# Gate products ahead of up products, the router's fold moved to GpSimd, and constant products in TensorE's waits

## The reference

```
mod = silu(c) @ W_ada + b_ada              -> shift, scale, gate, twice
h   = rms_norm(x)*(1+sc1) + sh1
u   = h @ W_in                             -> SSD group | MLA group
SSD : causal conv, SiLU, chunked scan (8 chunks of 128 tokens, 8 heads)
MLA : low-rank q and kv, rotary part, causal softmax attention, 8 heads
x   = x + g1 * rms_norm(concat(SSD, MLA) @ W_out)
h   = rms_norm(x)*(1+sc2) + sh2
router: group = argmax of 4 logits; the best 2 of that group's 8 experts
x   = x + g2 * rms_norm(sum over the 2 experts of
          w_e * (silu(h @ W_gate[e]) * (h @ W_up[e])) @ W_down[e])
```

## Time and profile before

| What | us |
|---|---|
| median of 3 runs | 1045.89 |
| fastest and slowest of them | 1043.03, 1046.33 |
| the profiled execution | 1050.27 |
| its span, first to last instruction | 1048.5 |
| TensorE busy in it | 954.7 |
| VectorE, ScalarE, GpSimd busy | 520.2, 302.3, 204.9 |

### The profile page before, as it was taken

The page is one execution under the profiler, slowest core; times in us unless marked ns, Lnnn a source line. Parts: engine busy times, 40 slices in busy tenths (PEclk is TensorE's granted clock), DMA queues, the critical chain, the costliest instruction groups (busy, mean ns, idle before and its releaser), DMA issues. The chain is left out here.

```text
span 1048.5 us, 12759 instructions
## 1 busy us (share of the span) xinstructions
PE 954.7 (91%) x4459; PEld 505.9 (48%) x4459; DVE 520.2 (50%) x961; ACT 302.3 (29%) x585; POOL 204.9 (20%) x247
## 2 busy tenths in 40 slices
PE   6999999999999999987999999748999998999946
PEld 4444444445466656666566665433333333333312
DVE  3366356444755555555578775662333332333327
ACT  3310001223443434432322322103333332333313
POOL 2200001223400600003343312011222221222003
PEclk9999999999989999998999999858999999999979
DMA  9986423000000000004011112995999999997547
GB/s 341 374 324 214 159 82 51 0 1 6 1 1 1 2 1 1 1 21 180 20 62 67 75 60 93 404 385 192 363 419 391 415 406 399 403 413 317 203 198 295
DMA packets 51815, 192.40 MB, mean 183 GB/s; under 512 B 15322, under 2 KB 20514, under 8 KB 36258
## 3 DMA queue, kind: packets, MB, share of 16 engines
q1 hardware_dynamic: 43396, 173.10, 42.6%
q0 software_dynamic: 7056, 18.36, 4.6%
q10 hardware_dynamic: 1296, 0.07, 0.1%
HBM read 174.21 MB, written 24.64 MB: 190 GB/s over the span
## 5 line engine op out<-in xcount | busy, mean ns | idle before, releaser
L1607 PE MATMUL PS<-ring,xg_T 128*64 x368 | 165.2, 603 | 3.5 <-ACT near_gu L1784 2.6
L1607 PE MATMUL PS<-near_gu,xg_T 128*64 128x512 f32 x368 | 165.2, 603 | 0.0
L1506 PE MATMUL PS<-w_out_sb,cat_T 128*128 128x512 f32 x256 | 120.8, 614 | 4.1 <-DVE y_sc L1927 2.8
L1003 PE MATMUL PS<-hT,w_x 128*128 128x512 f32 x256 | 111.6, 594 | 0.7 <-DMA w_x<-in_w_in_dram 0.7
L1607 PEld LDWEIGHTS PS<-ring,xg_T 128*64 128x64 f32 x368 | 51.1, 140 | 109.8 <-issue 109.8
L425 POOL TENSOR_SCALAR rstd<-stat 128x1 f32<-128x1 f32 (+1 forms) x48 | 21.9, 457 | 383.4 <-ACT junk L593 187.7
L1633 PE MATMUL PS<-ring,hid_T 128*64 x184 | 83.8, 598 | 0.4 <-DVE hid_T L2142 0.4
L1633 PE MATMUL PS<-near_dn,hid_T 128*64 128x512 f32 x184 | 83.9, 599 | 0.0
L2133 DVE TENSOR_TENSOR hid<-PS,hid_s 128x128 f32<-128x128 f32 x46 | 11.3, 286 | 145.9 <-ACT hid_s L1766 145.8
L898 DVE TENSOR_REDUCE row_max<-PS 128x1 f32<-128x1024 f32 (+7 forms) x64 | 48.2, 753 | 65.6 <-PE PS L1178 65.5
L1176 PE MATMUL PS<-kT,qT 96*128 96x512 f32 (+4 forms) x192 | 78.4, 519 | 0.0
(11 more groups left out here) (333 smaller groups left out, 1527.4 us busy)
## 6 DMA issues: line engine op xcount, KB each, us to landing
ring<-in_w_gate_dram SPq DMA_DIRECT2D x32, 1024.0 KB, 8.9
ring<-in_w_up_dram SPq DMA_DIRECT2D x32, 1024.0 KB, 11.7
ring<-in_w_down_dram SPq DMA_DIRECT2D x32, 1024.0 KB, 16.9
ada_later<-in_ada_w_dram SPq DMA_DIRECT2D x16, 1024.0 KB, 4.8
ada_first<-in_ada_w_dram SPq DMA_DIRECT2D x16, 512.0 KB, 10.7
y_g<-y_rows SPq DMA_DIRECT2D x8, 1024.0 KB, 12.4
x_in<-in_x_dram SPq DMA_DIRECT2D x8, 512.0 KB, 9.1
w_x<-in_w_in_dram SPq DMA_DIRECT2D x4, 1024.0 KB, 15.6
```

Source lines behind the costliest of these rows:

```text
L1003: last = pe.matmul(BANK[4 + n % 4][:, :], w_x[:, k, ct * P:(ct + 1) * P], hT[:, k, hh * HALF:(hh + 1) * HALF], start=(k == 0), stop=(k == ...
L1506: last = pe.matmul(BANK[6 + j], cat_T[t % 2][:, k, :], w_out_sb[:, k, j * HALF:(j + 1) * HALF], start=(k == 0), stop=(k == KC - 1))
L1607: last = pe.matmul(BANK[2 + b][rows_, :], xg_T[b][:, k, rows_], gu[u][:, :, k, :], start=(k == 0), stop=(k == KC - 1))
```

## The change

**The fold.** `router_columns`, `router_row` and their copies on VectorE are gone. GpSimd does the fold during attention, behind the chunk decays: the row times the identity, broadcast, and a tree of additions that leaves the diagonal as columns; the same with the 36 columns of the shift's product. What is left to TensorE is one product with `ones`, behind the first two products of the second block, and VectorE adds its result to the bias row there.

**Constant products.** `busy(bank, n)` issues n products of the identity with `ones` (128x128) into a bank that nothing reads before it is written again. In the lead-in there are 32 of them in six places, in the routing 105 in five (20, 4, 21, 24, 36).

**Gate and up.** `gate_up` does 16 products of 256 columns for gate into bank 2, and signals `gate_done`, then 16 for up into bank 3. SiLU waits for `gate_done`, the multiplication for `gu_done` as well. Both banks are now used by every tile; before, tiles took turns between two. So the next tile's gate waits for SiLU, and its up for the multiplication.

The diff (lists of semaphore names and unchanged lines left out):

```diff
@@ -213,6 +213,8 @@
+        fold = place("fold", R_U + 4096, [P, KC, P])
+        fold_r = place("fold_r", R_U + 4096, [P, KC, NG + E])
@@ -498,6 +500,22 @@
+            pool.wait_ge(S["w_r_loaded"], 32)
+            pool.wait_ge(S["mod_rows_ready"], 4 * (PARTS - 1))
+            for i, v in enumerate((B2, A2)):
+                link(pool.tensor_tensor(fold[:, :, :], v[:, :].rearrange("p (j k) -> p k j", k=KC), ident[:, :].unsqueeze(1).to_broadcast([P, KC, P]), ALU.mult))
+                n = P // 2
+                while n > 1:
+                    link(pool.tensor_tensor(fold[:, :, 0:n], fold[:, :, 0:n], fold[:, :, n:2 * n], ALU.add))
+                    n //= 2
+                link(pool.tensor_tensor(modc[:, i * KC:(i + 1) * KC].unsqueeze(2), fold[:, :, 0:1], fold[:, :, 1:2], ALU.add))
+            by_channel = lambda c0: modc[:, c0:c0 + KC].unsqueeze(2).to_broadcast([P, KC, NG + E])
+            link(pool.tensor_tensor(fold_r[:, :, :], w_r[:, :, :], by_channel(0), ALU.mult))
+            n = KC // 2
+            while n:
+                link(pool.tensor_tensor(fold_r[:, 0:n, :], fold_r[:, 0:n, :], fold_r[:, n:2 * n, :], ALU.add))
+                n //= 2
+            pool.tensor_tensor(w_r[:, :, :], w_r[:, :, :], by_channel(KC), ALU.mult).then_inc(S["fold_pool"], 1)
@@ -881,9 +899,6 @@
-                if hh == NH2 - 1:
-                    dve.wait_ge(S["fold_pe"], 1)
-                    dve.tensor_copy(modc[:, :], BANK[4][:, 0:2 * KC]).then_inc(S["fold_dve"], 1)
@@ -897,11 +912,6 @@
-                if st == 0:
-                    dve.wait_ge(S["fold_pe"], 2)
-                    dve.wait_ge(S["fold_dve"], 1)
-                    dve.tensor_tensor(rb_row[:, :], BANK[5][:, 0:NG + E], rb_row[:, :], ALU.add).then_inc(S["fold_dve"], 1)
-                    dve.tensor_tensor(w_r[:, :, :], w_r[:, :, :], modc[:, KC:2 * KC].unsqueeze(2).to_broadcast([P, KC, NG + E]), ALU.mult)
@@ -1087,22 +1097,6 @@
-            def router_columns():
-                pe.wait_ge(S["v_read"], NT - 1)
-                for i, v in enumerate((B2, A2)):
-                    for k in range(KC):
-                        last = pe.transpose(BANK[4][:, i * KC + k:i * KC + k + 1], v[0:1, k::KC], ident[0:1, 0:1])
-                last.then_inc(S["fold_pe"], 1)
-            def router_row():
-                pe.wait_ge(S["v_read"], NT)
-                pe.wait_ge(S["w_r_loaded"], 32)
-                pe.wait_ge(S["fold_dve"], 1)
-                for k in range(KC):
-                    last = pe.matmul(BANK[5][:, 0:NG + E], modc[:, k:k + 1].to_broadcast([P, P]), w_r[:, k, :],
-                                     start=(k == 0), stop=(k == KC - 1))
-                last.then_inc(S["fold_pe"], 1)
@@ -1145,10 +1139,7 @@
                         turned_query_pe(t - 1)
-                if hh == NH2 - 1:
-                    router_columns()
                 turned_query_pe((hh + 1) * NT // 2 - 1)
-            router_row()
@@ -1180,8 +1171,6 @@
-                    if g == 0:
-                        pe.wait_ge(S["fold_dve"], 2)
@@ -1424,6 +1413,13 @@
                 pe.matmul(BANK[7][:, 0:NH], ones[:, :], adt_f, start=True, stop=True).then_inc(S["cums_done"], 1)
+                pe.wait_ge(S["fold_pool"], 1)
+                pe.matmul(BANK[5][:, 0:NG + E], ones[:, :], fold_r[:, 0, :], start=True, stop=True).then_inc(S["fold_pe"], 1)
+
+                def busy(bank, n):
+
+                    for _ in range(n):
+                        pe.matmul(BANK[bank][:, 0:P], ident[:, :], ones[:, :], start=True, stop=True)
@@ -1484,6 +1480,8 @@
                     pe.wait_ge(S["cat_done"], t + 1)
+                    if t == 0:
+                        pe.wait_ge(S["fold_dve"], 1)
                     if t:
@@ -1526,13 +1524,20 @@
                 for t in range(-3, NT):
+                    if t == -2 or t == -1:
+                        busy(7, 6)
                     if tile(t + 2):
                         diagonal(t + 2)
+                    if t == -1:
+                        busy(7, 4)
                     if tile(t + 3):
...
                         decay_rows(t + 3, 0)
+                    if t == -2:
+                        busy(7, 7)
                     if t == -1:
                         cat_T_of(0)
+                        busy(7, 4)
                         pe.wait_ge(S["w_out_loaded"], 16)
@@ -1540,6 +1545,9 @@
                         h2_T_of(t)
+                    if t == -3:
+                        pe.wait_ge(S["cums_read"], 2)
+                        busy(7, 5)
                     if tile(t + 3):
@@ -1563,15 +1571,19 @@
                     .then_inc(S["rank_early"], 1)
+                busy(2, 20)
                 h2_T_of(NT - 1)
+                busy(2, 4)
                 route(NT - 1)
+                busy(2, 21)
                 pe.wait_ge(S["rt_both"], NT)
...
+                busy(5, 24)
                 for j in range(2):
@@ -1579,6 +1591,7 @@
                 last.then_inc(S["idx_done"], 1)
+                busy(5, 36)
@@ -1595,18 +1608,21 @@
-                    if n >= 2:
-                        pe.wait_ge(S["hid_done"], FC * (n - 1))
+                    if n:
+                        pe.wait_ge(S["silu_done"], n)
...
-                    for k in range(KC):
-                        for u in range(2):
-                            rows_ = slice(u * HT, (u + 1) * HT)
-                            last = pe.matmul(BANK[2 + b][rows_, :], xg_T[b][:, k, rows_], gu[u][:, :, k, :],
-                                             start=(k == 0), stop=(k == KC - 1))
-                    last.then_inc(S["gu_done"], 1)
+                    for s_ in range(2):
+                        if s_ and n:
+                            pe.wait_ge(S["hid_done"], FC * n)
+                        for k in range(KC):
+                            for u in range(2):
+                                rows_ = slice(u * HT, (u + 1) * HT)
+                                last = pe.matmul(BANK[2 + s_][rows_, 0:FF], xg_T[b][:, k, rows_], gu[u][:, s_, k, :],
+                                                 start=(k == 0), stop=(k == KC - 1))
+                        last.then_inc(S["gu_done" if s_ else "gate_done"], 1)
@@ -1760,10 +1776,10 @@
-                    act.wait_ge(S["gu_done"], n + 1)
+                    act.wait_ge(S["gate_done"], n + 1)
...
-                    act.activation(hid_s[b][:, :], BANK[2 + b][:, 0:FF], ACT.Silu).then_inc(S["silu_done"], 1)
+                    act.activation(hid_s[b][:, :], BANK[2][:, 0:FF], ACT.Silu).then_inc(S["silu_done"], 1)
@@ -1841,6 +1857,8 @@
                 dve.tensor_tensor(flat(dec_out), flat(tot), flat(acs), ALU.subtract).then_inc(S["cums_read"], 1)
+                dve.wait_ge(S["fold_pe"], 1)
+                dve.tensor_tensor(rb_row[:, :], BANK[5][:, 0:NG + E], rb_row[:, :], ALU.add).then_inc(S["fold_dve"], 1)
@@ -2129,8 +2147,9 @@
+                    dve.wait_ge(S["gu_done"], n + 1)
...
-                        dve.tensor_tensor(hid[b][:, k, :], BANK[2 + b][:, FF + k:2 * FF:FC], hid_s[b][:, k::FC], ALU.mult)\
+                        dve.tensor_tensor(hid[b][:, k, :], BANK[3][:, k:FF:FC], hid_s[b][:, k::FC], ALU.mult)\
...

```

4 lines of the change are left out of this document (2 added, 2 removed).

## The result

| Kernel | Median us | Runs | Lowest, highest |
|---|---|---|---|
| before, same chip | 1046.11 | 4 | 1043.03, 1047.66 |
| changed | 1033.63 | 4 | 1033.11, 1034.08 |

The ratio is 0.987, 95% interval 0.9851 to 0.9889. So the change is worth 12.5 us by the medians, 13.6 us by the ratio and 11.6 to 15.6 us by its interval, where 17.9 were forecast. The time of 1033.63 lies inside the stated range of 1021 to 1038, and at the slow end of the 1022 to 1034 that I gave the mechanism by itself.

The account below looks back on a forecast made before the run. TensorE was taken as the bound, interrupted by per-tile handovers, tile 13's transfer and half-clock stretches. -6.5 (attention), -1.4 (lead-in), -5.3 (routing), -4.7 (tiles) make -17.9, so 1045.89 becomes 1028.0 us; range 1021 to 1038.

Parts of the forecast that it names:

- Attention's start: Opening of attention: earlier scores at full clock, first transposes of probabilities at 301.9; -6.5 us, bounds -4.0 and -7.
- The anchor: The 17.9 us gain, set against the profiled execution's 1050.27, was taken off the runs' median 1045.89, giving 1028.0 us.
- The lead-in: Ahead of the projection: constant products fill TensorE's waits and raise the clock; -1.4 us, bounds +1.3 and -2.5.
- The routing: Router to tile 0's gate and up: constant products keep full clock; -5.3 us, bounds -2 and -7.
- The table's start: In the routing, behind choice and ranks: products outlast the choice by 0.6 us, ranks are done 3.1 earlier.
- the gather: Ahead of tile 0: up to 3 us longer beside experts 4 and 5; transposes 1.2 to 2.8 earlier, 2.0 taken.
- The tiles: Expert tiles: SiLU hidden behind up, 0.4 us gained per tile (0.15 to 0.5); sum -4.7 us, bounds -2 and -8.
- Tile 13: Held by expert 21's transfer: its wait grows from 2.6 to about 6 us, and the late clock costs +0.5.
- The first: Lead-in and routing: products outlast the waits by as much as they win; gain 10, 1036 us; chance 0.14.
- The second: Gate and up: narrow passes cost extra, taking 7.74 us, a tile loses 0.36; gain 7.5, 1038 us; chance 0.08.
- the third: Tiles up to 13: transfers do not hold tile 13, thirteen tiles give 5.2 us; gain 24, 1022 us; chance 0.12.
- The fourth: Lead-in and routing: constant products do not raise the clock, passes take 0.213 us; 18 slower, 1064 us; chance 0.04.

Follow-up runs that it names:

- the two comparisons: The changed kernel against the kernel before, unedited, on two chips: 1033.63 against 1046.11 us, then 1033.13 against 1048.75 us (ratio 0.9848).
- the version with everything together: Changed kernel plus VectorE adding the last tile's B2, expert 5's load behind gather and landing signals, 31 constant products instead of 36: 1027.89 us, ratio 0.9806.

## Why the prediction was right, and where its sizes were wrong

The direction, the range and the mechanism of the three parts held. The size did not: 17.9 us forecast, 12.5 and 15.6 by the medians of the two comparisons, 13.6 and 15.9 by their ratios. What the mean over the traces gives by stage, as worked out below, is 3.7 for attention's start, 2.5 for the lead-in, 4.2 for the routing with tile 0, 1.0 from there to tile 14 and 3.1 behind it, 14.5 in all.

**Attention's start** is the term that was mis-sized. I put -6.5 us, and the two traces differ by 6.3, at full clock, just as worked out (297.3 and 301.9 forecast, 297.45 and 302.02 seen). But the trace before was an extreme one. Over the five traces with the old opening the first transposes start between 305.07 and 308.36, 306.2 as a mean, and over the nine with the fold between 301.92 and 303.35, 302.5 as a mean. The step is worth 3.7 us, 2.8 less than I took and less than my lower bound of 4.0. That bound assumed a clock that stays low after the edit, and in five of the nine traces it is low for a part of the stretch; that the stretch before was not always as slow as in the one trace I had, I didn't consider.

**The anchor** failed with it. I worked out the gain against an execution that stood 4.4 us above its kernel's median and took the whole of it off the median. What made that execution slow was half clock in attention's start and in the lead-in, and the change removes half clock there. The lower median should have cost me some of the gain.

**The lead-in** gave 2.9 us between the two traces, and 2.5 as a mean over the traces (30.1 us in the five with the old one, 27.6 in the nine with the constants, of which the one with constants alone is one). I took 1.4. I had put 1.9 us against it for products that outlast their waits, and they hardly do: behind three of the six groups TensorE still waits, 0.20 to 0.38 us, and the wait ahead of the projection fell from 1.28 to 0.38.

```profile
487.50 1.06 PE L1422 MATMUL PS<-ones,ident 128*128 128x128 f32 x8
488.94 3.67 PE L1504 MATMUL PS<-w_out_sb,cat_T 128*128 128x512 f32 x8 [0.38 <-ACT cat_T L1719]
```

**The routing** gave 4.0 instead of 5.3, and 4.2 as a mean over traces (40.8 us in five with the old one, 36.6 in the three of the constants and the whole change). The transposes, the router and tile 0 came as reckoned (2.5 for 2.7, and 2.0 for 2.2), and the table gave 1.6 for 1.0. Two terms failed. The table's start was to come 0.4 sooner still after the router's passes, and came 0.3 later, because of the 1.07 us that VectorE lost beside GpSimd. That an earlier choice would run beside GpSimd's addition could be read from the trace before; I did not read it. And the gather took 2.5 us more. I had "up to 3 us longer" as a bound. The gather's issue came 3.7 us sooner (4.1 forecast), the transposes 1.2 (2.0 forecast, and 1.2 its lower end).

**The tiles**: 0.35 us each for 0.4. Gate and up rose by 0.02, not 0.09, so the narrow passes cost next to nothing. My estimate of what is late next was wrong in kind. I named the multiplication, and it is TensorE's four transposes (0.64 us), which I had as hidden. The Trainium skill, in "TensorEngine Tiling (Array Packing)", section "Instruction Overhead", puts some 60 cycles on every matmul. As a cost that adds up over passes the trace disagrees, since 64 passes of 256 columns took 6.91 us and 32 of 512 took 6.89.

**Tile 13** is where transfers held before, and with the gate's edit tile 11 is a second such place. From the end of tile 0's gate and up, when the first reload is issued, to tile 13 it takes 155.94, 156.50, 155.94 and 156.63 us in the four traces without the gate's edit and 155.2 to 155.5 in nine of the ten with it (the tenth, at 158.2, is the version with everything together). So the twelve tiles between, which save 4.2 us of TensorE, gave some 0.9, where I had 1.2. The waits ahead of them grew from 2.6 to 6.3 us, as reckoned ("about 6 us in all"), but only in part where I had put them: 2.3 to 2.7 us of wait stand ahead of tile 11 in nine of the ten traces with the edit, and in none without it. Tile 13 itself, which was to save 0.4 and lose 0.5 to the clock, grew by 1.0 us in the pair above. That is the clock of one trace (gate and up 9.84 us there, 8.81 in the second trace of the whole change): to tile 14 it takes 13.8 to 14.1 us in the four traces without the edit, 13.5 to 13.7 in six with it, 14.6 and 14.75 in two (the pair's among them), and 12.0 in two. From the end of tile 0's gate and up to tile 14 the edit gives 1.0 us as a mean.

**The rivals.** The first (clock held only in part) came nearest in its time, 1036, but not by its mechanism: behind seven of the eleven groups TensorE still waits, 0.20 to 0.97 us, and both lead-in and routing became shorter. The second fell with the 6.91 us and the third with the 155 us; the third's own terms, added up, make 25.8 and not 24. The fourth fell with the passes at 0.11 to 0.12 us in every group of the routing.

## What to carry to other kernels

Where a change removes stretches of half clock, take several executions of the kernel before, since one trace may hold more of such stretches than the median run, and the gain must be reckoned against the same execution that anchors the time. Work that fills TensorE's waits can pay for itself though it computes nothing, if it ends where the wait ends; when a stage comes sooner, look at what it will now run beside, on the neighbouring engine and among the transfers. A new wait in a queue that also passes on other engines' signals goes behind those signals.

## What the runs showed of the hardware

- VectorE beside GpSimd: an operation on 128x4 took 1.29 to 1.31 us in six traces while GpSimd added 128x1024 numbers, and 0.22 where that addition was over or gone.
- A gather of tile 0's rows took 4.7 to 4.8 us alone (four traces) and 6.3 to 7.9 us while a 3 MB expert was coming in (five).
- Constant passes of 128 columns take 0.115 us each (8.30 / 72), and 64 passes of 32 columns 2.06 us at full clock, 32 ns each; at half clock they had taken 57.
- One kernel's runs on one chip spread over 8.6 us (1044.44 to 1053.08, 20 runs) with the mean clock between 0.964 and 0.952. The changed kernel's eight runs lie between 1032.01 and 1035.67, at 0.979 to 0.983.
